# The input projection of a streaming encoder layer, asked for in 24 parts and carried out in whole pieces of four

## What is computed

```python
proj = rmsnorm(xf, norm_mix_g) @ w_in                  # (rows, 1024) @ (1024, 2208)
p_mla, p_rw = proj[..., :MLA_COLS], proj[..., MLA_COLS:]
c, kr = mla_kv_rows(p_mla, pos, ...)                   # latents and shared key
qn, qr = mla_queries(p_mla, pos, ...)
r, w, k, v, kk, a, gl = rwkv_inputs(p_rw, prev, ...)   # needs the row before each row
def step(S, inp):                                      # the RWKV-7 state, in chunks of 64 rows here
    sa = jnp.einsum('bhvk,bhk->bhv', S, -kk_t)
    S = S * w_t + sa[..., None] * (kk_t * a_t) + v_t[..., None] * k_t
    return S, jnp.einsum('bhvk,bhk->bhv', S, r_t)
```

## Time and profile before

| | |
|---|---|
| median of 3 runs | 2313.56 us (2300.03 to 2319.51) |
| the profiled execution | 2318.96 us, its span 2317.2 us |
| mean granted TensorE clock | 0.917 |
| TensorE busy | 2095.0 us (90%) |
| VectorE busy | 993.3 us (43%) |
| GpSimd busy | 571.6 us (25%) |
| ScalarE busy | 348.0 us (15%) |

### The profile page before, as it was taken

The page is one execution under the profiler, slowest core; times in us unless marked ns, Lnnn a source line. Parts: engine busy times, 40 slices in busy tenths (PEclk is TensorE's granted clock), DMA queues, the critical chain, the costliest instruction groups (busy, mean ns, idle before and its releaser), DMA issues. The chain is left out here.

```text
span 2317.2 us, 33421 instructions
## 1 busy us (share of the span) xinstructions
PE 2095.0 (90%) x14049; PEld 1583.2 (68%) x14049; DVE 993.3 (43%) x1801; ACT 348.0 (15%) x818; POOL 571.6 (25%) x380
## 2 busy tenths in 40 slices
PE   6699889888898876799997799799999999989999
PEld 3356666566665665566765466688888888868887
DVE  1456655655556563431313623433343333432522
ACT  1122212222122221122121200100011100000000
POOL 2433432424324231000001300211221221153342
PEclk9799989999899987797876899799999999999999
DMA  9443442444324100310100030211111111223332
GB/s 353 136 132 126 134 128 97 140 136 138 111 98 151 44 20 15 88 37 23 32 5 24 29 130 32 88 37 37 55 37 37 55 37 37 78 81 108 113 123 66
DMA packets 74399, 193.84 MB, mean 84 GB/s; under 512 B 20026, under 2 KB 48266, under 8 KB 67219
## 3 DMA queue, kind: packets, MB, share of 16 engines
q1 hardware_dynamic: 66914, 114.94, 15.4%
q10 hardware_dynamic: 7344, 76.88, 9.4%
HBM read 163.10 MB, written 20.44 MB: 79 GB/s over the span
## 5 line engine op out<-in xcount | busy, mean ns | idle before, releaser
L1946 PE MATMUL psum<-mixT,wA 128*128 128x264 f32 x1408 | 338.2, 388 | 6.3 <-DVE mixT L2133 4.8
L327 PE MATMUL psum<-wsl,xt 128*128 128x368 f32 x864 | 322.6, 516 | 6.8 <-ACT proj L656 6.3
L1946 PE MATMUL psum<-u_sum,wA 128*128 128x264 f32 x1232 | 300.2, 389 | 7.9 <-POOL wA L2086 7.9
L1946 PEld LDWEIGHTS psum<-mixT,wA 128*128 128x128 f32 x1408 | 269.1, 191 | 53.3 <-issue 5.3
L1946 PEld LDWEIGHTS psum<-u_sum,wA 128*128 128x128 f32 x1232 | 236.1, 192 | 48.9 <-POOL wA L2086 8.0
L327 PEld LDWEIGHTS psum<-wsl,xt 128*128 128x128 f32 x864 | 166.0, 204 | 107.0 <-issue 25.6
L2084 POOL TENSOR_TENSOR wA<-wA 128x512 f32<-128x512 f32 x22 | 27.9, 1266 | 402.9 <-DMA wA<-in_w_gate 206.7
L1946 PE MATMUL psum<-hid,wA 128*128 128x264 f32 x528 | 121.5, 386 | 2.1 <-DVE hid L2201 1.5
L1929 PE MATMUL psum<-mixT,hid 128*128 128x352 f32 x384 | 115.8, 465 | 4.3 <-DMA hid<-in_w_out 4.3
L1946 PEld LDWEIGHTS psum<-hid,wA 128*128 128x128 f32 x528 | 100.2, 190 | 19.9 <-issue 2.8
L1929 PEld LDWEIGHTS psum<-mixT,hid 128*128 128x128 f32 x384 | 73.9, 193 | 45.7 <-DMA hid<-in_w_out 4.5
(11 more groups left out here) (354 smaller groups left out, 3027.6 us busy)
## 6 DMA issues: line engine op xcount, KB each, us to landing
wsl<-in_w_in ACTq DMA_DIRECT2D x51, 1472.0 KB, 6.7
wA<-in_w_down SPq DMA_DIRECT2D x32, 704.0 KB, 4.0
wA<-in_w_gate SPq DMA_DIRECT2D x22, 512.0 KB, 4.1
wA<-in_w_up SPq DMA_DIRECT2D x22, 512.0 KB, 4.1
mixed<-proj SPq DMA_DIRECT2D x8, 784.0 KB
xt<-in_x_tiles SPq DMA_DIRECT2D x9, 512.0 KB, 10.9
wsl<-in_w_in SPq DMA_DIRECT2D x3, 1472.0 KB, 13.7
hid<-in_x_cols SPq DMA_DIRECT2D x1, 4224.0 KB, 14.4
```

What stands on the lines that cost most here:

```text
L327: return pe.matmul(out, lhsT, rhs, start=start, stop=stop)
L1946: ins = pe.matmul(pb[bank][:, 0:NW], left(k), right(k), start=first and k == 0, stop=k == depth - 1, skip_group_check=not first)
```

## The change

`Fill` keeps what it is asked for in a count `owed` and issues only whole pieces of four parts: a call adds n to the count, and issues the multiple of four that the count holds. `rest` issues what is left of the 24. The calls stay where they are.

```diff
@@ class Fill @@
             def __init__(self, p):
-                self.p, self.u, self.means = p, 0, 0
+                self.p, self.u, self.means, self.owed = p, 0, 0, 0
 
             def __call__(self, n):
                 if self.p >= TILES:
+                    return
+                self.owed += n
+                n, self.owed = self.owed // 4 * 4, self.owed % 4
+                if not n:
                     return
                 p, b = self.p, self.p % 2
                 if self.means:
@@
             def rest(self):
-                self(4 * IPC - self.u)
+                self(4 * IPC - self.u - self.owed)
```

## The result

The changed kernel takes 2361.93 us (median of 4 runs, 2346.04 to 2366.03) against 2316.03 of the kernel before in the same rounds: 1.0199 times as long, with a 95% interval of 1.0131 to 1.0267, or +46 us. Forecast was 2374 in a range of 2336 to 2402. The profiled execution took 2359.64 us, its span 2357.9, which is 40.7 more than the span before. Up to the first matmul of the attention phase the two traces are 46.3 us apart (936.89 against 983.17). The phases behind it, whose instructions are the same in both, ran 5.6 us shorter in this execution; no run explains that, and it isn't used.

The account below looks back on a forecast made before the run. TensorE was taken as the bound, busy 86.41 of 95.00 us a turn. Seven turns of 7.4 idle plus 1.5 clock, less 2 for the opening, give +60 us: 2374 against the median 2313.56, range 2336 to 2402.

Parts of the forecast that it names:

- part A: From `scores_b` to `level_ed` 0: VectorE sets the length, so two parts less there leave +2.67 us idle a turn.
- parts B and D: `level_t` 1 to `level_ed` 1, +0.86 us; `T1h` 3 to `state_in` 0, +3.1 with bare links of 0.86, 0.79, 0.78.
- part C: Wait for the low-rank transposes: more of VectorE's 7.12 us lies bare, +0.8 us a turn, between 0 and +1.8.
- part D: `T1h` 3 to `state_in` 0: four parts fewer, VectorE sets the end, +3.1 us idle a turn, between +2.4 and +4.0.
- Idle time in sum: TensorE's added idle time over a turn with a projection: 7.4 us, between 5.9 and 9.3.
- The sum of the work is zero: Same 864 records issued, 16 parts moved within a turn; only idle time and clock change its time. A piece costs 5.33 us.
- The clock: TensorE's lower clock at `level_ed` 0 and some on the transposes: +1.5 us a turn, between 0 and +3.
- third slow stretch: A new lower-clock stretch expected behind the 3.4 us wait at `level_ed` 0, costing 0.8 on each half of it.
- the second one: Existing lower-clock stretch of turn 3, 480 to 492 us, mean clock 0.57, behind the 2.05 us wait; costs 5.2 a turn.
- The opening part: Before the turns: small products go out ahead of the projection after waits for VectorE; -2 us, between -4 and +1.
- The clock gains from whole pieces: Rival: sixteen records in a row keep the clock up at the 480 to 492 stretch; about 2332 us; chance 0.12.
- The links go out earlier: Rival: solve links hand over 1.8 us sooner each and waits shrink, a turn wins 6.9, 2265 us; chance 0.05.

Follow-up runs that it names:

- the run of pieces 4, 5 and 0: Against the kernel before, only pieces 4, 5 and 0 of a tile issued whole, the others in their old parts: 1.0008 times, +2 us.
- The run of pieces 2 and 3 alone: Against the kernel before, only pieces 2 and 3 issued whole, the others in their old parts: 1.0046 times, +11 us.
- with spare matmuls: Unread matmuls put into TensorE's waits, no real work moved: kernel before 0.9821 (2274.96 us), changed kernel 1.0027 (2321.20 us), both against the kernel before.
- the three partial kernels: Kernel before with only some pieces issued whole: 4, 5 and 0 (1.0008); 1 (0.9948); 2 and 3 (1.0046).
- piece 1 alone: Against the kernel before, only piece 1 issued whole, the others in their old parts: 0.9948 times, 11 us faster.
- two parts moved: Kernel before with the F(1) behind the low-rank transposes and the F(1) behind lora made one F(2) ahead of those transposes: 0.9804, 2268.79 us.

## Why the prediction was right, step by step

- **VectorE's stretch of 12.98 us (part A).** Right as stated: start to start it is 14.62 us in both turns seen and in the kernel before, with two parts less in it now. The 2.02 ahead of `scores_k`, the end of the wait for the level masks and the 3.4 at `level_ed` 0 came (3.56) where the clock was up. Where it was down the same stretch holds slow work for idle time, so the idle time of this part is over-stated by about half (9.1 for 18.7 in the run of pieces 4, 5 and 0), while its length is not.
- **Bare links (parts B and D).** 0.86, 0.86, 0.79 and 0.79, from the turn without a projection: to the hundredth or the next.
- **The low-rank transposes (part C).** +0.8 forecast, +1.1 and +0.8 in the two turns seen (4.43, 4.12). Over turns 0 to 6 it is 3.35 to 5.09, so between nothing and +1.7, +1.0 in the mean: near the middle of the stated range, and not steady.
- **`T1h` 3 to `state_in` 0 (part D).** 18.39 us for a forecast 18.15, `keys` 7.35 behind `T1h` as in turn 7, and 3.05 of waiting where 2.7 was expected. The run of pieces 2 and 3 alone gave +22.4 us of idle time, 21.7 forecast.
- **Idle time in sum.** 52 forecast, 45.4 measured, less because slow work stands in part of it. At the upper clock a turn's idle time grew by 7.9 (turn 4 of the changed kernel, 17.10 against 9.16) and by 8.9 (with spare matmuls), above the 7.4 and inside 5.9 to 9.3.
- **"The sum of the work is zero".** This did not hold. The prediction priced a piece at four times a part, 5.33, and it takes 5.15 or less in one run; a turn with whole pieces has 1.4 to 1.7 us less work at the upper clock, 10 to 12 in seven. That the length of the turn at the clock of 1.00 grew by 7.46 for a forecast 7.4 is luck: 8.9 of idle time less 1.4 of work.
- **The clock.** +1.5 a turn forecast, 10 in all. The busy time grew by 8.2, but from work that is some 10 smaller, so by this estimate the lower clock added about 18, near the upper end of the stated 0 to 3 a turn. It made up for the work that the prediction had too high, and for idle time that slow work took the place of. The picture behind it is right only in part. The third slow stretch at `level_ed` 0 came in five of seven turns, and in turn 1 as forecast, behind a wait of 3.58 (1.97 for a half of `level_ed`). In four it began earlier, in the piece ahead, and in turn 4 it was absent behind a wait of 3.56 (1.15 and 1.10). And the second one wasn't kept: it now lies at `state_in` 0 to the piece behind it (0.51 from 492 to 502), and `cum` runs at full clock in turn 3. A sum of stretches at fixed places was the wrong model, as the three partial kernels show: by it each would have been slower by its idle time at least.
- **The opening part.** -2 forecast; -4.6 with 2.7 of it from an earlier first matmul, so -1.9.
- **The rivals.** "The clock gains from whole pieces" is what happened with piece 1 alone, at about the 5.2 us a turn that it was priced with, but not in the whole change. The Trainium skill's page "Perfetto Trace Analysis", section "Matmul Optimizations", asks for batches back to back. Runs of 16 records were seen with 0.87, 0.91, 0.96 and 1.00 of the clock, so here the length of a run alone decided neither the clock nor the time. "The links go out earlier" did not come: the long waits grew.
- **The number.** 2374 forecast, 2361.93 measured; a turn of 104.5 forecast, 103.7 in the mean of turns 1 to 5. Place and idle time are right by mechanism. The close sum owes something to errors that cancel, of work and of clock.

## What to carry to other kernels

In a queue that is carried out in order, filler work is worth what its place covers. Read the price of each place from a stretch of the trace in which the filler is missing anyway (here the turns at the end), and ask for each long wait which filler could stand ahead of it: two parts moved gave 48 us, where rounding to whole pieces cost 46. About 19 of the 48 were idle time, and 26 the lower clock. Idle time adds up over places, and single links came as read to 0.1 us, whole turns to within 1.5. Filler in one run is less work than the same filler in pieces (77.2 against 78.9 us a turn), so ask for both: few runs, at the places that wait. The lower clock of TensorE doesn't add up, so test single changes with the clock held, and don't infer the value of one part of a change from its own run alone.

## What was not expected of the hardware

- The same matmuls in fewer, longer runs are less work: with the clock at 1.00, 77.17 us of busy time in a turn with six runs of 16 records, 78.91 in one with fifteen shorter runs, and 5.15 us for a piece in one run where two halves take 5.34. No run shows which part of a change from one set of matmuls to the next takes that time.
- Whether a slow stretch comes in a turn is decided by more than the waits right ahead of it. With piece 1 whole, the waits of 2.05 and 0.66 us ahead of `cum` were unchanged, there was 1.9 us more of waiting in the turn, and the granted clock between 384 and 394 us was 1.00, where it was 0.57 before. What it is that decides isn't settled by these runs.
- Matmuls whose result nobody reads, 100 records of them, made the kernel before 41 us faster (0.9821).
- Work at the lower clock inside a stretch that another engine sets costs nothing: 6.91 and 5.21 us for the same piece, with 1.87 and 3.56 us of waiting behind it, and 14.62 us from `scores_b` to `level_ed` 0 in both.
